# Two filler products per attention unit taken out of the hybrid mixer of a two-block model

## What is computed

```python
for l in range(2):                                   # first block
    x = layer_norm(ALPHA * x + 0.5 * swiglu(x, ...))
    h = split_columns(x @ w_in[l])
    y_a = mla_mixer(...)       # causal softmax attention, 4 heads, 96-wide q and k
    y_b = nsa_mixer(...)       # per head: compressed keys (31), selected keys, window keys, gated sum
    y_c = dsa_mixer(...)       # index scores pick the 128 best keys of a query (top_k), then attention
    y_d = stick_breaking_mixer(...)
    x = layer_norm(ALPHA * x + group_norm(y_a, y_b, y_c, y_d) @ w_out[l])
    x = layer_norm(ALPHA * x + 0.5 * swiglu(x, ...))
x = second_block(x, ...)                             # state space model, gated recurrence, swiglu
```

## Time and profile before

| | |
|---|---|
| median of the timed runs | 3993.78 us (3992.47 to 4023.08) |
| span of the profiled execution, first to last instruction | 3995.3 us |
| TensorE busy with products | 3604.5 us, 90% of the span |
| VectorE, ScalarE busy | 1782.0 us (45%), 1451.4 us (36%) |
| mean granted TensorE clock over the span | 0.939 |
| attention phase, first score product to last values product | 605.9 to 809.3 us (layer 1), 1919.5 to 2095.3 us (layer 2) |

### The profile page before, as it was taken

One profiled execution on the slowest core, in us unless ns is written; L12 is line 12 of the kernel. 1 busy time (PEld: TensorE's weight loads), 2 busy tenths in 40 slices (PEclk: granted clock), 3 DMA queues, 4 the chain that ended last, 5 costly groups with the idle time before them and its releaser, 6 DMA issues. The chain is left out here.

```text
span 3995.3 us, 44743 instructions
## 1 busy us (share of the span) xinstructions
PE 3604.5 (90%) x16162; PEld 2815.3 (70%) x16200; DVE 1782.0 (45%) x2970; ACT 1451.4 (36%) x2379; POOL 48.8 (1%) x44
## 2 busy tenths in 40 slices
PE   7999989988999899988998899958888897889998
PEld 6877657766888688866677687836676675667876
DVE  3333458435332433344864433265655446534333
ACT  4322425353332433242545332244544335323322
POOL 0000020000000000001000000000000000000000
PEclk9999998688999899999898999979999998999999
DMA  3332210002332123221001233211121122222331
GB/s 134 95 106 72 99 44 1 1 27 69 96 105 88 64 94 101 88 88 60 1 1 37 70 99 102 82 33 44 53 64 59 58 79 66 73 70 90 94 104 59
DMA packets 73728, 276.78 MB, mean 69 GB/s; under 512 B 10368, under 2 KB 11904, under 8 KB 72832
## 3 DMA queue, kind: packets, MB, share of 16 engines
q1 hardware_dynamic: 73600, 275.12, 21.1%
HBM read 272.99 MB, written 2.10 MB: 69 GB/s over the span
## 5 line engine op out<-in xcount | busy, mean ns | idle before, releaser
L341 PE MATMUL ps<-xh,whi 128*128 128x512 f32 x2880 | 1151.1, 400 | 166.4 <-DVE xl L482 70.2
L342 PE MATMUL ps<-xl,whi 128*128 128x512 f32 x2880 | 1135.2, 394 | 0.0
L343 PE MATMUL ps<-xh,wlo 128*128 128x512 f32 x2880 | 1134.0, 394 | 0.0
L313 DVE TENSOR_TENSOR wlo<-raw,whi 128x1024 fp32r<-128x1024 f32 (+2 forms) x464 | 602.4, 1298 | 1075.4 <-ACT whi L309 1075.4
L341 PEld LDWEIGHTS ps<-xh,whi 128*128 128x128 f32 x2880 | 549.4, 191 | 311.7 <-issue 142.1
L309 ACT ACTIVATE whi<-raw 128x1024 fp32r<-128x1024 f32 (+2 forms) x464 | 514.7, 1110 | 509.4 <-PE ps L343 501.4
L343 PEld LDWEIGHTS ps<-xh,wlo 128*128 128x128 f32 x2880 | 549.6, 191 | 117.7
L342 PEld LDWEIGHTS ps<-xl,whi 128*128 128x128 f32 x2880 | 550.9, 191 | 112.6 <-issue 2.4
L341 PE MATMUL ps<-ffn_hh,whi 128*128 128x512 f32 x880 | 350.6, 398 | 12.6 <-DVEq L607 12.6
L343 PE MATMUL ps<-ffn_hh,wlo 128*128 128x512 f32 x880 | 349.8, 397 | 0.0
L342 PE MATMUL ps<-ffn_hl,whi 128*128 128x512 f32 x880 | 349.7, 397 | 0.0
(11 more groups left out here) (327 smaller groups left out, 3940.0 us busy)
## 6 DMA issues: line engine op xcount, KB each, us to landing
raw<-in_ffn_up SPq DMA_DIRECT2D x216, 512.0 KB, 3.5
raw<-in_ffn_down SPq DMA_DIRECT2D x80, 704.0 KB, 4.0
raw<-in_mix_in SPq DMA_DIRECT2D x40, 512.0 KB, 3.5
raw<-in_ssm_in SPq DMA_DIRECT2D x40, 512.0 KB, 3.6
raw<-in_lru_in SPq DMA_DIRECT2D x20, 512.0 KB, 3.5
raw<-in_mix_out SPq DMA_DIRECT2D x16, 512.0 KB, 3.2
raw<-in_ssm_out SPq DMA_DIRECT2D x12, 512.0 KB, 3.7
raw<-in_lru_out SPq DMA_DIRECT2D x8, 640.0 KB, 3.9
```

The lines of the kernel that those rows point to most:

```text
L313: dve.tensor_tensor(self.core.wlo[:, u % HALF, 0:width], self.core.raw[:, u, 0:width], self.core.whi[:, u % HALF, 0:width].bitcast(F32), A ...
L341: pe.matmul(out, c.whi[:, h, w], xh[:, k0 + k], start=first and k == 0, stop=False)
L342: pe.matmul(out, c.whi[:, h, w], xl[:, k0 + k], start=False, stop=False)
L343: mm = pe.matmul(out, c.wlo[:, h, w], xh[:, k0 + k], start=False, stop=last and k == nk - 1)
```

## The change

The two filler products in `transposes` go, and with them the helper. Nothing else is touched: waits, buffers, order of the rest, all other engines' code.

```diff
-def keep_clock(c, pe, bank, n):
-    for _ in range(n):
-        pe.matmul(c.ps[:, bank], c.kb["ident"], c.kb_all[:, 0:SEQ], start=True, stop=True, skip_group_check=True)
...
                     if u >= 2:
                         pe.wait_ge(ph["pt_done"], u - 1)
-                    keep_clock(c, pe, 6 + u % 2, 2)
                     pe.wait_ge(ph["exp_done"], u + 1)
```

## The result

The changed kernel takes 4041.11 us (median of 4 runs, 4039.18 to 4048.04), the kernel before 3993.12 us in the same session (4 runs, 3990.07 to 4023.08). The ratio is 1.0154, with a 95% interval of 1.0106 to 1.0202. Predicted were 4060 us and a range of 4028 to 4098. The ratios of this text leave out every run that is more than 1.5% above the fastest of its kernel, so a ratio need not be the quotient of the two medians beside it.

What follows compares the result with a forecast made beforehand. TensorE was taken to bound the fourth NSA head and, at 1.2 GHz, set the pace; VectorE bounds MLA heads. NSA +7 and +30, DSA +10 and +15, MLA +4 sum to +66 us: 4060 us, range 4028 to 4098.

Steps and rivals of the forecast that it cites:

- The forecast case: Attention phases: clock falls within the first NSA units in both layers, stays down to phase end; 4060 us, chance 0.72.
- Filler at 1.2 GHz, 0.43 us each, all on the path: Fourth NSA head at the lower clock: removing 24 filler products saves 10.3 us, leaving 29.5 of 39.8 us.
- Item 1: Four NSA heads per layer without filler, mostly at the lower clock: 120.5 us, +7 in layer 1, +30 in layer 2.
- the two don't overlap fully: First three NSA heads: TensorE's and VectorE's work overlap only partly, so 31 us each rather than 29.5.
- Item 2: DSA units without filler at the lower clock: 48 us, +10 in layer 1 and +15 in layer 2.
- The factor between the levels: DSA units: slowdown from upper to lower clock lies between 1.69 and 2, giving 44 to 53 us.
- Item 3: MLA heads: clock rises some 5 us later without filler, +2 us a layer, bounds 0 and +16.
- a shorter TensorE stream can gain almost nothing there: MLA heads: VectorE is busy 7.50 of 7.50 us, so a head at the upper clock stays at 7.5 us.
- the clock holds: Rival for both attention phases: clock stays at the upper level without filler, together −57, 3937 us; chance 0.06.
- the filler doesn't decide: Rival: clock pattern stays as before, down in layer 1 from 711.8 to 776.6 us; −38, 3956 us; chance 0.07.
- MLA stays down too: Rival: MLA heads also at the lower clock, 11.5 us instead of 7.5, +32 instead of +4, 4088 us; chance 0.10.
- Down in one layer only: Rival: clock falls in just one layer, half of the sums, some 4000 to 4020 us; chance 0.05.

Runs made afterwards that it cites:

- e7_fourth1: Kernel before with filler products only in NSA heads: two per unit, three in the third head, one in the fourth; 3951.67 us, ratio 0.9874.
- e9_fourth1_again: Repeat of e7_fourth1, the same kernel in more rounds; 3949.68 us (7 runs), ratio 0.9919 to the kernel before.
- e2_rows32: Kernel before with its two filler products per unit on 32 of the array's 128 rows, same 512 columns; 4260.85 us, ratio 1.0712.
- e1_one: Kernel before with one filler product per unit instead of two; 4043.39 us, ratio 1.0187.
- e8_dsa_only: Kernel before with its two filler products per unit kept in the DSA units alone, none in MLA and NSA; 4030.76 us, ratio 1.0136.
- e4_mla_none: Kernel before with filler left out of the MLA units alone, kept in NSA and DSA; 3969.3 us, ratio 0.9995.

## Why the prediction was right, and where its terms were off

The forecast case came: the clock at 0.50 from the first NSA head to the end of DSA in both layers, TensorE the bound, no change elsewhere. VectorE's busy time in the two phases stayed (135.4 and 135.5 us, 136.1 and 136.3 before), and its idle time before its last step of a unit grew from 28.8 to 58.6 us in layer 2 and from 56.9 to 59.3 in layer 1 (waits for the values products), as the prediction said it would. The sum said +66 us on the profiled span, the profiles show +42.4, the timed medians +48.0. The whole stands near the low end: all lower bounds together give 4039 us (3994 + 66 − 9 − 8 − 4), which is above the 4028 that the prediction wrote as the end of its range.

- **Filler at 1.2 GHz, 0.43 us each, all on the path**: right. The fourth head was put at 29.5 us and took 29.9 and 30.0.
- **Item 1, the first three heads**: mis-sized. They were put at 31 us each less 2 us for the first stretch, a layer at 120.5 us; measured 112.9 and 112.3. The step that failed is "the two don't overlap fully". The second and third heads take 30.0 and 29.9 us with VectorE's search, as the fourth does without it, and TensorE has no gap in them. That the three units of scores in stock even out short and long units is the likely reason; no run changed that number. And the stretch at the upper level saved not 2 but some 7 us: the clock held for 7.6 and 8.9 us into the first NSA head, which took 23.1 and 22.5 us. The item's lower bound, 29.5 us a head, was the better value, and with the longer first stretch the item came out below its bound: instead of +7 and +30 it was −0.4 and +21.6, 16 us less in all, where the bound allowed 9.
- **Item 2, DSA**: nearly right. 48 us were forecast on the windows of the earlier trace rows, which end 1.2 us after the last DSA score; the 45.6 us measured end at it. Cut there, the kernel before has

```profile
765.30:802.30 37.00, 36.62 (x203) 27.57 (x206) 14.20 (x65) 13.89 (x46) 0.00 (x0) 0.85 0.00 1
2056.40:2088.20 31.80, 31.59 (x202) 23.99 (x205) 14.20 (x65) 14.40 (x46) 0.00 (x0) 1.00 0.00 1
```

so the change is +8.6 and +13.8. What follows the cut, the last units' values, adds +2.8 and +2.6: the last values product of layer 1 starts 9.8 us after the last DSA score now (813.4 − 803.6), and 7.0 us before (809.3 − 802.3).

```profile
L1044 PE MATMUL ps<-mix_tok_sb,att_pt x240: 285/421/422, 652.6 to 813.4; 128*128 128x64 f32 x120
```

Together +28 where the sum had +25. The factor between the levels is 45.6 / 25.4 = 1.80, in the middle of the bounds 1.69 and 2. The lower bound itself was too low, since the 17.5 us it divides by hold some waiting: 29.9 us against 20.80 − 18 × 0.21 = 17.0 us (e7_fourth1's fourth head, whose window has 18 filler products) is 1.76.

- **Item 3, MLA**: sign wrong, size small. Forecast was +2 a layer; from the first MLA score to the first NSA score it is 44.0 and 44.4 instead of 46.1 us in both layers, −2. The step "a shorter TensorE stream can gain almost nothing there" failed for the last MLA head, which in the kernel before was

```profile
644.50:652.00 7.50, 7.45 (x51) 5.60 (x51) 6.47 (x33) 4.45 (x14) 0.00 (x0) 1.00 0.01 3
```

with VectorE busy 6.47 of 7.50 us and TensorE 7.45: TensorE was the bound there, and I had read only the head before it. Now the head takes 6.70 us, with VectorE busy all of it. That is 0.8 of the 2.1 us of layer 1; 1.1 us more are saved before the second MLA head's first score (22.4 instead of 23.5 us); the kernel before had its first filler products there, from 628.8 us on, while the clock was still at 0.50. And the clock rises 24.2 us after the first MLA score in layer 1 (24.0 before) and 26.0 us in layer 2 (24.4 before), not 5 us later: at once in layer 1 and 1.6 us later in layer 2.
- **Sum of the parts**: layer 1's phase from the first MLA score to the last values product goes from 203.4 to 212.3 us, layer 2's from 175.7 to 212.0, together +45.2. By items that is −3.8 for MLA (forecast +4), +21.2 for NSA (+37), and +27.8 for DSA and its end (+25). The rest of the program is 2.8 us shorter; that is less than the rest differs from one profile to the next of the same kernel, 3620.9 us in e7_fourth1 and 3615.1 us in e9_fourth1_again.
- **The rivals**: "the clock holds" is excluded by the profile, "the filler doesn't decide" by the same, and by the filler counts (none, one, two, three), with which the place of the fall moves, "MLA stays down too" did not come in the changed kernel but did in e2_rows32, which shows what it costs: 47.2 − 24 × 0.56 = 33.8 us for three MLA heads less their filler, 11.3 us each, where the prediction had 11.5. "Down in one layer only" is how the kernel before was profiled.
- **The clock as a matter of chance in the kernel before**: the prediction read the fall at 711.8 us as a sign that these units stand at an edge. The timed runs agree, as far as times and mean clocks can show it: over 19 runs of one group the kernel before goes from 3963.48 to 4026.17 us, and over 13 of another the granted clock goes from 0.949 at 3963.69 us to 0.929 at 4023.67, while the four runs of the changed kernel keep within 9 us, at mean clocks of 0.904 to 0.906.

The Trainium skill was cited twice ("TensorE: Matmul & The Clock Gate"). The table "Why this matters for your kernels" of that page of the Trainium skill, which asks for no long idle gaps between products, would have given a clock that holds. The changed kernel's NSA heads, with TensorE busy 29.90 of 29.90 us at 0.50, and e2_rows32 speak against this as a sufficient rule. The statement of the Trainium skill (Part 4 of the same page) that transposes count less stays unshown.

## What to carry to other kernels

Before filler work is taken out of an engine, look at the granted clock with it in and ask in which stretches it holds the clock, not how long it takes: here 320 products of 0.21 us were worth more than they cost, although none stood at a place where it was needed for the result. The opposite also holds: at the lower level filler is pure cost, so the slowest kernels are those with filler that doesn't reach its aim: e1_one in part (4043 us, no better than without filler), e2_rows32 in full (4261 us). Place it where another engine is the bound and TensorE's waits can hide it, leave it out where the real products keep the clock by themselves, and repeat the timing: a clock at the edge shows as a spread between runs, not in one profile.

## What the runs showed of the hardware that was not expected

- To keep the clock takes less than to get it back. The DSA units keep 1.00 without filler of their own (26.00 us, e7_fourth1), but do not raise it from 0.50 in 45.6 us (changed kernel). With two products a unit it comes back after about 19 us (e8_dsa_only), and after 11 us in layer 1 of the kernel before; with one, after 19 us in layer 2 of e1_one and not within the DSA units in layer 1. The fourth NSA head with two products is the same: it keeps 1.00 (22.6 us, e4_mla_none) and doesn't raise 0.50 in 39.8 us.
- Filler products on 32 rows did not raise the clock in any unit (e2_rows32, 0.50 from the first of them to the end of the phase), and at 0.50 a 512-column one costs 0.56 us in its place between products on more rows, against 0.43 us for one on 128 rows.
- The factor between the two levels is not 2 for real work: 45.6 / 25.4 = 1.80 for the DSA units and 29.9 / 17.0 = 1.76 for the fourth NSA head, both without filler (the divisors are the estimates above).
